# Turns without convolution matmuls behind the scores, and a merge stage written out with its adds moved forward

## The chip, the cores and the metric

The kernel runs on one core of one Trainium2 chip. The metric is the device time of one launch in microseconds; the median of three runs is quoted. A profiled execution has a span, from its first to its last instruction, and a device time of its own, which is a little longer.

## The reference, cut to what matters

One layer of a diffusion backbone over 512 latent tokens and 256 context tokens, model width 1024, all in float32:

```python
h = modulate(rmsnorm(x, norm1_g), sh1, sc1)          # shifts, scales, gates = silu(c) @ w_ada + b_ada
p = h @ w_in                                         # kv | rope key | q | conv x | conv B | conv C | gates
o = mla_latent(qn, qr, keys, rope_keys, values)      # 8 heads, 768 keys, softmax
y_conv = (b_gate * dwconv(c_gate * x_in, conv_w, conv_b)) @ w_conv_out
y_attn = o @ w_attn_out
x = x + g1 * ((sigmoid(gate_attn) * y_attn + sigmoid(gate_conv) * y_conv) @ w_o)
x = x + g2 * conv_ffn(modulate(rmsnorm(x, norm2_g), sh2, sc2), w_up, ffn_conv_w, ffn_conv_b, w_down)
return rmsnorm(x, final_g)
```

The change touches the stage in which attention and the convolution branch (`y_conv` up to the product with `w_conv_out`) run together, and the stage behind it, the gated merge, in which the later shifts, scales and gates (columns of `w_ada` from 2048 on) are summed as well.

## The kernel before, in words

Every product is made of three matmuls (`mm3`, L365 to L369): each operand is split into a rounded part (`hi`) and a rest (`lo`), and hi*hi, lo*hi and hi*lo are summed. Weights come in units of 128 x 1024: SyncE (SP) loads a unit into one of two `raw` buffers, ScalarE (ACT) makes `whi` (`split_hi`, L297), GpSimd (POOL) makes `wlo` (`split_lo`, L306; the subtraction is L311) in one of four slots, TensorE (PE) uses it and counts `w_used`. ACT may split a unit when the one four before it has been used.

**Attention with the convolution.** The 8 heads have 4 query tiles each: 32 turns g, head h = g // 4, tile t = g % 4. In turn g PE does in this order (L1421 to L1439): in turns 3, 11 and 19 first two products that make the keys of the next pair of heads (`keys`), then the scores of turn g + 2 (`scores`; they need the exponential of two turns earlier, since two pairs of banks take turns), a piece of a convolution projection (`conv_piece`, L1403), a third or so of a head's output (`output`, 6 matmuls), and the transposes of the probabilities of turn g (`transposes`, L1387; they need the normalised probabilities and the `lo` halves of turn g - 1). VectorE (DVE) does the maximum (L1011) and the bias (L1013) of turn g + 2, the normalisation (L1018, L1020) of turn g + 1, and the `lo` halves (`ptlo`, L1057 and L1060) of turn g; ACT the `hi` halves (`pthi`, L750 and L753) of turn g, then the exponential (L708) of turn g + 2, then, in some turns, output parts (L716, L721) and a weight split.

The convolution runs beside it in four groups of eight turns, one for each 128 channels. A group has three projections of 24 matmuls, all into PSUM bank 7. Which turn does how many is in `CONV_PIECES` (L84). Between them the bank has to be emptied: `conv_x_copy` on ACT (L726) after the first, `conv_product` on DVE (L1031) after the second, `conv_gate` on DVE (L1045) after the third; `conv_mid` (ACT, L731) and `conv_taps` (DVE, L1035 and L1038) make the depthwise convolution in between. PE waits in `conv_piece`, at the first matmul of each projection, for the copy, the product or the gate before it. `SPLIT_AT` (L85) says behind which turns ACT and POOL split the units of the convolution and the first three of the merge.

**Merge.** For each of 8 blocks d PE does three units of 24 matmuls (L1445 to L1477): the two gates and the two branch outputs. ACT makes the sigmoids (L787), DVE the products (L1096), their sum (L1101), ACT the sum's `hi` copy (L790), DVE its `lo` rest (L1104). ACT has the split of a later unit behind each of the three steps, so also behind its wait for the sum. DVE does four adds of the modulation sum ahead of each block's products (`ada2_add`, L1071; L1080 for the first row block, L1083 after it), each on half a megabyte that SP loads into one of two buffers (`ada2`); SP alternates these loads with those of the next block's units (`load_ada2`, `gate_load`). The loads of `w_o` come behind the last of them. Blocks 0 to 3 are written out, blocks 4 to 7 are a loop with one iteration. Behind the merge PE does the first tile of the product with `w_o`, its last eighth held back until `mlo` of block 7 is there (L1506), and then sums the rows of `adacc` with a matmul by ones (`mod_rows`, L1482).

Of the kernel before, what the change touches and what calls it, by code (L numbers as in the profile page):

```python
# [26 lines left out]
P = 128  # L27
D = 1024
# [55 lines left out]
CONV_PIECES = ((0, 8), (0, 8), (0, 8), (1, 8), (1, 8), (1, 8), (2, 12), (2, 12))  # L84
# [3 lines left out]
def build(nc, x, c, ctx, c_ctx, w_ada, b_ada, norm1_g, w_in, q_norm_g, kv_norm_g, w_uq, w_ukv, conv_w,  # L88
# [3 lines left out]
    with stack:  # L92
# [3 lines left out]
        def sb(name, shape, dt=F32, scope=stack):  # L96
            return scope.enter_context(nc.sbuf_tensor(name, shape, dt))
# [63 lines left out]
        ada2 = sb("ada2", [P, 2, D], scope=mrg)  # L161
        sb("gap2", [P, 1536], scope=mrg)
# [226 lines left out]
        def _(sp):  # L389
# [50 lines left out]
            def load_ada2(n, k, g):  # L440

                wait(sp, s("ada2_used"), n - 1)
                if not isinstance(n, int):
                    sp.sem_inc(s("load_turn"), 1)
                rows = w_ada[k * P:(k + 1) * P, :] if isinstance(k, int) else w_ada[bass.ds(k * P, P), :]
                sp.dma_start(ada2[:, g % 2, :], rows[:, (2 + g) * D:(3 + g) * D]).then_inc(s(f"ada2_loaded{g % 2}"), 16)
# [148 lines left out]
        def _(act):  # L595
# [147 lines left out]
            for g in range(HEADS * TT):  # L743
# [19 lines left out]
                if g % 8 == 2:  # L763
                    conv_x_copy(g // 8)
# [9 lines left out]
            def merge_hi(i, first):  # L774
                for dd in range(4):
                    d = 4 * i + dd
                    b = 4 * (dd % 2)
                    for n in range(3):
                        m = 3 * dd + n
                        if n < 2:  # L780
                            used(act, U_MERGE + 3 * d + n)
                            if first and dd == 0:
                                act.wait_ge(s("z_lo"), CT)
                                act.wait_ge(s("o_lo"), HEADS)
                            if not (first and dd < 2):
                                act.wait_ge(s("m_lo"), d - 1)
                            nc.scalar.activation(work[:, 3 * (dd % 2) + n, :], ps[:, b + n, :], ACT.Sigmoid).then_inc(s("g_sig"), 1)  # L787
                        else:
                            act.wait_ge(s("m_sum"), d + 1)
                            nc.scalar.activation(at1(mhi, d), work[:, 3 * (dd % 2) + 2, :], ACT.Copy).then_inc(s("m_hi"), 1)  # L790
                        split_hi(act, U_MERGE + 12 * i + m + 4, m % SLOTS)

            merge_hi(0, True)
            with act.Fori(1, 2) as i:
                merge_hi(i, False)
# [91 lines left out]
        def _(dve):  # L887
# [183 lines left out]
            def ada2_add(n, k, g):  # L1071

                gg = g * D
                if isinstance(n, int):
                    dve.wait_ge(s(f"ada2_loaded{g % 2}"), 16 * (n // 2 + 1))
                else:
                    dve.wait_ge(s(f"ada2_loaded{g % 2}"), (n - g % 2) * 8 + 16)
                cv = cvec[:, k, 0:1] if isinstance(k, int) else cvec[:, bass.ds(k, 1), 0:1].rearrange("p a b -> p (a b)")
                if isinstance(k, int) and k == 0:
                    nc.vector.tensor_scalar(adacc[:, gg:gg + D], ada2[:, g % 2, :], cv, None, ALU.mult).then_inc(s("ada2_used"), 1)  # L1080
                else:
                    dve.wait_ge(s("ada2_used"), n - 3)
                    nc.vector.scalar_tensor_tensor(out=adacc[:, gg:gg + D], in0=ada2[:, g % 2, :], scalar=cv,  # L1083
                                                   in1=adacc[:, gg:gg + D], op0=ALU.mult, op1=ALU.add).then_inc(s("ada2_used"), 1)


            def merge_lo(i, first):
                for dd in range(4):
                    d = 4 * i + dd
                    b, w = 4 * (dd % 2), 3 * (dd % 2)  # L1090
                    for m in range(4):
                        ada2_add(4 * d + m, d, m)
                    for n in range(2):
                        used(dve, U_MERGE + 3 * d + 2)
                        dve.wait_ge(s("g_sig"), 2 * d + n + 1)
                        nc.vector.tensor_tensor(out=work[:, w + n, :], in0=ps[:, b + 2 + n, :], in1=work[:, w + n, :],  # L1096
                                                op=ALU.mult).then_inc(s("m_prod"), 1)
                    dve.wait_ge(s("m_prod"), 2 * d + 2)
                    if not (first and dd < 2):
                        dve.wait_ge(s("m_lo"), d - 1)  # L1100
                    nc.vector.tensor_tensor(out=work[:, w + 2, :], in0=work[:, w, :], in1=work[:, w + 1, :],  # L1101
                                            op=ALU.add).then_inc(s("m_sum"), 1)
                    dve.wait_ge(s("m_hi"), d + 1)
                    nc.vector.tensor_tensor(out=at1(mlo, d), in0=work[:, w + 2, :], in1=at1(mhi, d).bitcast(F32),  # L1104
                                            op=ALU.subtract).then_inc(s("m_lo"), 1)

            merge_lo(0, True)
            with dve.Fori(1, 2) as i:
                merge_lo(i, False)
# [117 lines left out]
        def _(pe):  # L1227
# [195 lines left out]
            for g in range(HEADS * TT):  # L1423
# [6 lines left out]
                conv_piece(g)  # L1430
# [14 lines left out]
            def merge(i, first):  # L1445
                for dd in range(4):
                    d, b = 4 * i + dd, 4 * (dd % 2)
                    if first and dd == 0:

                        pe.wait_ge(s("p_exp"), HEADS * TT)  # L1450
                    if first and dd == 1:
                        pe.wait_ge(s("pt_lo"), HEADS * TT)
                        pe.wait_ge(s("o_val"), HEADS)
                        pe.wait_ge(s("c_z"), CT)
                    if not (first and dd < 2):
                        pe.wait_ge(s("m_prod"), 2 * d - 2)
                    for n in range(2):
                        m = 3 * dd + n
                        pe.wait_ge(w_lo, U_MERGE + 12 * i + m + 1)
                        project(pe, ps[:, b + n, :], m % SLOTS, hhi, hlo).then_inc(w_used, 1)  # L1460
                    m = 3 * dd + 2
                    slot = m % SLOTS
                    pe.wait_ge(w_lo, U_MERGE + 12 * i + m + 1)
                    if first and dd == 0:
                        pe.wait_ge(s("z_lo"), CT)
                        pe.wait_ge(s("o_lo"), HEADS)
                    for k in range(CT):
                        mm3(pe, ps[:, b + 2, :], (tile_of(whi, slot, k), tile_of(wlo, slot, k)),
                            (qhi[:, 2 * k, :], qlo[:, 2 * k, :]), k == 0, k == CT - 1)
                    for k in range(CT):  # L1470
                        last = mm3(pe, ps[:, b + 3, :], (tile_of(whi, slot, CT + k), tile_of(wlo, slot, CT + k)),
                                   (qhi[:, 2 * k + 1, :], qlo[:, 2 * k + 1, :]), k == 0, k == CT - 1)
                    last.then_inc(w_used, 1)

            merge(0, True)
            with pe.Fori(1, 2) as i:
                merge(i, False)  # L1477
# [181 lines left out]
```

## Time and profile before

| | us |
|---|---|
| median of 3 runs | 907.83 (905.94 to 908.05) |
| the profiled execution | 908.06 |
| its span | 906.3 |

| stage, us from the span's start | PE busy | granted clock |
|---|---|---|
| 45 to 137, projections, queries, values | 77.39 of 92 | 0.91 |
| 137 to 329, attention and convolution | 167.23 of 192 | 0.92 |
| 329 to 350, merge | 21.00 of 21 | 1.00 |
| 350 to 395, merge | 45.00 of 45 | 1.00 |
| 395 to 465, merge and the first tile of w_o | 68.88 of 70 | 1.00 |
| 533 to 770, up projection | 236.69 of 237 | 1.00 |

The page gives over the whole span: PE busy 834.3 us (92%), DVE 498.8 (55%), ACT 377.0 (42%), POOL 368.7 (41%). Busy time says little by itself: one looks for the stages in which PE has gaps or a clock under 1, and then for what ended those gaps. In the rows below, "[2.45 <-DVE tab L1045]" behind an instruction says that its engine sat idle for 2.45 us before it and that DVE's instruction of line 1045 ended that wait. The rounded clock of a stretch mixes the two levels, 2.4 GHz (1.00) and 1.2 GHz (0.50).

### The profile page before, as it was taken

The page shows a single profiled execution, that of the slowest core. Times are in us where ns is not written, and L with a number is a line of the kernel's source. Part 1 is how long each engine was busy: PE and PEld are TensorE (multiplying, and loading weights), DVE is VectorE, ACT ScalarE, POOL GpSimd, SP SyncE. Part 2 cuts the span into 40 slices and gives each one's busy share as a digit, 9 for nine tenths or more (in the row PEclk, how much of TensorE's full clock was granted, in tenths as well). Part 3 has the DMA queues.
Part 4 walks back from the last instruction along what each step waited for, and adds up shares of the span by engine and source line. Part 5 has one row for each costly group of instructions (what it writes and reads, how often), then busy time and mean ns, then how long its engine had stood idle before and what let it go on. Part 6 is the DMA issues. An engine that isn't in the chain of part 4 may idle for free.

```text
span 906.3 us, 11419 instructions
## 1 busy us (share of the span) xinstructions
PE 834.3 (92%) x3960; PEld 685.9 (76%) x3960; DVE 498.8 (55%) x604; ACT 377.0 (42%) x577; POOL 368.7 (41%) x187
## 2 busy tenths in 40 slices
PE   6679969888888799999989989999999999999995
PEld 4458757777777688888857888888888888888884
DVE  5862898776767637877631486655555555100014
ACT  7763445445444442322132445444444444221134
POOL 0193455232433255554453314544444444444420
PEclk9989989999999899999999989999999999999998
DMA  8822212010110138877544213333333332332202
GB/s 313 279 64 53 59 36 71 24 47 24 35 37 24 47 117 250 234 230 237 171 135 160 70 48 93 116 93 93 95 106 100 93 93 93 108 102 93 93 24 93
DMA packets 126238, 96.21 MB, mean 106 GB/s; under 512 B 13468, under 2 KB 111033, under 8 KB 126201
## 3 DMA queue, kind: packets, MB, share of 16 engines
q1 hardware_dynamic: 126169, 95.71, 34.9%
q8 instruction: 23, 0.38, 0.2%
q14 instruction: 14, 0.11, 0.0%
q10 hardware_dynamic: 32, 0.01, 0.0%
HBM read 93.60 MB, written 2.10 MB: 106 GB/s over the span
## 4 chain that ended last, share of the span: by engine, by line
PE 63%; issue 12%; DVE 10%; POOL 6%; DMA 3%; ACT 3%; SPq 1%; POOLq 0%; ACTq 0%; DVEq 0%
PE ps L367 17%; PE ps L369 17%; PE ps L368 17%; PE ps L1416 7%; POOL wlo L311 5%; DVE small L1013 2%; PE ps L1398 2%; PE ps L1387 2%; DMA raw<-w_in_dram 2%; DVE work L988 1%; DVE small L1011 1%; PE ps L1482 1%; POOL ht L511 1%; DVE work L992 1%; DMA xt<-x_dram 1%
## 5 line engine op out<-in xcount | busy, mean ns | idle before, releaser
L311 POOL TENSOR_TENSOR wlo<-raw,whi 128x1024 fp32r<-128x1024 f32 (+2 forms) x130 | 299.7, 2311 | 478.5 <-ACT whi L303 478.4
L367 PE MATMUL ps<-hhi,whi 128*128 128x512 f32 (+1 forms) x552 | 213.3, 386 | 9.0 <-DVE hlo L928 5.8
L368 PE MATMUL ps<-hlo,whi 128*128 128x512 f32 (+1 forms) x552 | 211.9, 384 | 0.0
L369 PE MATMUL ps<-hhi,wlo 128*128 128x512 f32 (+1 forms) x552 | 211.6, 383 | 0.0
L303 ACT ACTIVATE whi<-raw 128x1024 fp32r<-128x1024 f32 (+2 forms) x131 | 127.5, 982 | 129.5 <-PE ps L369 86.7
L367 PEld LDWEIGHTS ps<-hhi,whi 128*128 128x128 f32 x552 | 105.6, 191 | 30.2 <-issue 3.7
L369 PEld LDWEIGHTS ps<-hhi,wlo 128*128 128x128 f32 x552 | 105.6, 191 | 20.1
L368 PEld LDWEIGHTS ps<-hlo,whi 128*128 128x128 f32 x552 | 105.7, 191 | 19.9 <-issue 0.2
L1189 DVE SCALAR_TENSOR_TENSOR work<-ps,prm,work 128x511 f32<-128x511 f32 x44 | 33.0, 749 | 73.5 <-ACT work L851 72.6
L1083 DVE SCALAR_TENSOR_TENSOR adacc<-ada,cvec,adacc 128x1024 f32<-128x1024 f32 x28 | 64.9, 2336 | 14.2 <-DMA ada<-w_ada_dram 14.2
L367 PE MATMUL ps<-fhi,whi 128*128 (+1 forms) x176 | 69.2, 393 | 0.1
L369 PE MATMUL ps<-fhi,wlo 128*128 (+1 forms) x176 | 68.6, 390 | 0.0
L368 PE MATMUL ps<-flo,whi 128*128 (+1 forms) x176 | 68.5, 389 | 0.0
L1212 DVE SCALAR_TENSOR_TENSOR x2T<-ps,mod,x2T 128x512 f32<-128x512 f32 x8 | 6.0, 750 | 107.3 <-PE ps L369 107.3
L851 ACT ACTIVATE work<-ps,prm 128x512 f32<-128x512 f32 x44 | 34.2, 778 | 70.8 <-PE ps L369 70.8
L1416 PE MATMUL ps<-hhi,whi 128*128 128x512 f32 x96 | 44.0, 458 | 20.9 <-DVE work L1031 10.4
L750 ACT ACTIVATE pthi<-ps 128x512 fp32r<-128x512 f32 x32 | 19.1, 598 | 85.9 <-PE ps L1387 85.9
L1198 DVE TENSOR_TENSOR work<-work 128x512 f32<-128x512 f32 x22 | 44.3, 2012 | 8.0 <-ACT work L856 4.2
L1057 DVE TENSOR_TENSOR ptlo<-ps,pthi 128x512 fp32r<-128x512 f32 x32 | 22.0, 687 | 46.4 <-ACT pthi L750 46.4
L1416 PEld LDWEIGHTS ps<-hhi,whi 128*128 128x128 f32 x96 | 21.1, 220 | 29.4 <-issue 24.7
L1416 PE MATMUL ps<-hlo,whi 128*128 128x512 f32 x96 | 42.9, 447 | 0.0
L1416 PE MATMUL ps<-hhi,wlo 128*128 128x512 f32 x96 | 42.3, 441 | 0.0
(235 smaller groups left out, 1477.9 us busy)
## 6 DMA issues: line engine op xcount, KB each, us to landing
raw<-w_up_dram SPq DMA_DIRECT2D x88, 256.0 KB, 3.1
raw<-w_in_dram SPq DMA_DIRECT2D x66, 256.0 KB, 3.4
ada<-w_ada_dram SPq DMA_DIRECT2D x32, 512.0 KB, 4.2
raw<-w_down_dram SPq DMA_DIRECT2D x44, 256.0 KB, 2.7
adaraw<-w_ada_dram SPq DMA_DIRECT2D x32, 256.0 KB, 4.9
raw<-w_o_dram SPq DMA_DIRECT2D x16, 256.0 KB, 3.2
xt<-x_dram SPq DMA_DIRECT2D x4, 512.0 KB, 6.4
raw<-w_attn_out_dram SPq DMA_DIRECT2D x8, 256.0 KB, 2.9
```

Source lines behind the costliest of these rows:

```text
L303: ins = nc.scalar.activation(h, r, ACT.Copy)
L311: ins = (engine or nc.gpsimd).tensor_tensor(out=l, in0=r, in1=h.bitcast(F32), op=ALU.subtract)
L367: pe.matmul(o, l[0], r[0], start=start, stop=False)
L368: pe.matmul(o, l[0], r[1], start=False, stop=False)
L369: return pe.matmul(o, l[1], r[0], start=False, stop=stop)
L750: nc.scalar.activation(pthi[:, 0:4, t * P:(t + 1) * P], ps[:, 4, :].rearrange("p (k n) -> p k n", n=P), ACT.Copy).then_inc(s("pt_hi"), 1)
L851: nc.scalar.activation(work[:, 3 * jj + n, :], ps[:, 2 * jj + n, :], ACT.Identity, bias=col(prm, R_FB + n * FT + j), scale=col(prm, R_FW + ...
L1057: nc.vector.tensor_tensor(out=ptlo[:, 0:4, t * P:(t + 1) * P], in0=ps[:, 4, :].rearrange("p (k n) -> p k n", n=P), in1=pthi[:, 0:4, t * P: ...
L1083: nc.vector.scalar_tensor_tensor(out=adacc[:, gg:gg + D], in0=ada2[:, g % 2, :], scalar=cv, in1=adacc[:, gg:gg + D], op0=ALU.mult, op1=ALU ...
L1189: nc.vector.scalar_tensor_tensor(out=u[:, 1:T], in0=p[:, 0:T - 1], scalar=col(prm, R_FW + n * FT + j), in1=u[:, 1:T], op0=ALU.mult, op1=AL ...
L1198: nc.vector.tensor_tensor(out=work[:, 3 * jj + 2, :], in0=work[:, 3 * jj, :], in1=work[:, 3 * jj + 1, :], op=ALU.mult).then_inc(s("f_prod" ...
L1416: last = pe.matmul(ps[:, 7, :], tile_of(wlo if term == 2 else whi, u % SLOTS, k), (hlo if term == 1 else hhi)[:, k, :], start=i == 0, stop ...
```

## The change

`CONV_PIECES` becomes 12, 12, 0, 12, 12, 0, 24, 0 matmuls, and a turn with 0 skips the call. The bank is emptied in other turns: the copy on ACT behind turn 1 (was 2), the product on DVE at the end of turn 4 (was 5), the taps at the end of turn 6 (as before), the gate at the beginning of turn 7, ahead of that turn's maximum (was at its end). In the merge stage PE, ACT and DVE have their blocks written out instead of half of them in a loop; SP was written out already. The adds of the modulation sum are spread 5, 5, 5, 5, 4, 4, 4, 0 over the blocks instead of four for each, in the same order, and `ada2` has three buffers in place of two.

```diff
-CONV_PIECES = ((0, 8), (0, 8), (0, 8), (1, 8), (1, 8), (1, 8), (2, 12), (2, 12))
+CONV_PIECES = ((0, 12), (0, 12), (0, 0), (1, 12), (1, 12), (1, 0), (2, 24), (2, 0))
+ADA_ADDS = (5, 5, 5, 5, 4, 4, 4, 0)
...
-        ada2 = sb("ada2", [P, 2, D], scope=mrg)
-        sb("gap2", [P, 1536], scope=mrg)
+        ada2 = sb("ada2", [P, 3, D], scope=mrg)
+        sb("gap2", [P, 512], scope=mrg)
...
+            def load_ada2(n):
+
+                k, g = n // 4, n % 4
+                wait(sp, s("ada2_used"), n - 2)
+                sp.dma_start(ada2[:, n % 3, :], w_ada[k * P:(k + 1) * P, (2 + g) * D:(3 + g) * D]).then_inc(s(f"ada2_loaded{n % 3}"), 16)
...
             for d in range(DT):
-                for g in range(4):
-                    load_ada2(4 * d + g, d, g)
-                    if g < 3 and d + 1 < DT:
-                        gate_load(d + 1, g)
+                for m in range(max(3, ADA_ADDS[d])):
+                    if m < ADA_ADDS[d]:
+                        load_ada2(sum(ADA_ADDS[:d]) + m)
+                    if m < 3 and d + 1 < DT:
+                        gate_load(d + 1, m)
...
-                if g % 8 == 2:
+                if g % 8 == 1:
                     conv_x_copy(g // 8)
...
+            for d in range(DT):
+                b, w = 4 * (d % 2), 3 * (d % 2)
+                for n in range(3):
+                    m = 3 * d + n
+                    if n < 2:
+                        used(act, U_MERGE + m)
...
+                        nc.scalar.activation(work[:, w + n, :], ps[:, b + n, :], ACT.Sigmoid).then_inc(s("g_sig"), 1)
+                    else:
+                        act.wait_ge(s("m_sum"), d + 1)
+                        nc.scalar.activation(mhi[:, d, :], work[:, w + 2, :], ACT.Copy).then_inc(s("m_hi"), 1)
+                    split_hi(act, U_MERGE + m + 4, m % SLOTS)
...
             for g in range(HEADS * TT):
                 h, t = g // TT, g % TT
+                if g % 8 == 7:
+                    conv_gate(g // 8)
                 if g + 2 < HEADS * TT:
                     maxima(g + 2)
...
-                if g % 8 in (5, 6, 7):
-                    (conv_product, conv_taps, conv_gate)[g % 8 - 5](g // 8)
+                if g % 8 == 4:
+                    conv_product(g // 8)
+                if g % 8 == 6:
+                    conv_taps(g // 8)
...
+            def ada2_add(n):
+
+                k, gg = n // 4, n % 4 * D
+                dve.wait_ge(s(f"ada2_loaded{n % 3}"), 16 * (n // 3 + 1))
...
+            for d in range(DT):
+                b, w = 4 * (d % 2), 3 * (d % 2)
+                for m in range(ADA_ADDS[d]):
+                    ada2_add(sum(ADA_ADDS[:d]) + m)
+                for n in range(2):
+                    used(dve, U_MERGE + 3 * d + 2)
...
-                conv_piece(g)
+                if CONV_PIECES[g % 8][1]:
+                    conv_piece(g)
...
```

## Rows read from the trace of the kernel before

**Rows 1.** Windows by stage: us, busy time of each engine, PEclk, DMA share, GB/s.
```profile
137.00:329.00 192.00, 167.23 (x903) 141.84 (x902) 135.69 (x219) 91.68 (x171) 66.45 (x34) 0.92 0.14 36
...
350.00:395.00 45.00, 45.00 (x200) 37.28 (x199) 37.75 (x23) 13.42 (x17) 26.64 (x9) 1.00 0.80 238
```

**Rows 2.** The same columns for one group of eight turns.
```profile
231.80:279.46 47.66, 42.06 (x228) 35.59 (x229) 34.59 (x56) 23.02 (x43) 17.19 (x10) 0.93 0.13 34
```

**Rows 3.** Waits of PE, 137 to 329: total us, times, longest.
```profile
PE ps L1416 <- DVE work L1031: 10.4, 4, 3.4
PE ps L1416 <- DVE tab L1045: 7.4, 3, 2.5
PE ps L1416 <- ACT work L726: 3.1, 1, 3.1
```

**Rows 4.** Chain that ended last, in attention: start, us, what.
```profile
184.20 3.59 PE ps L1416 x8
187.79 0.72 PE ps L1398 x6
...
195.19 1.83 PE ps L1416 x8
```

**Rows 5.** Timeline of turns 8 and 9: start, us, engine, line, operation.
```profile
188.35 0.82 PE L1387 MATMUL ps<-ident,work 128*128 128x128 f32 x6
...
189.72 0.28 PE L367 MATMUL ps<-khi,qhi 96*128 96x256 f32 x1
...
190.78 0.39 PE L1416 MATMUL ps<-hhi,wlo 128*128 128x512 f32 x1
```

**Rows 6.** Timeline from transposes of turn 9 to the scores behind the keys.
```profile
192.60 0.82 PE L1387 MATMUL ps<-ident,prob 128*128 128x128 f32 x6
...
196.93 2.40 POOL L311 TENSOR_TENSOR wlo<-raw,whi 128x1024 fp32r<-128x1024 f32 x1 [12.18 <-ACT whi L303]
...
197.44 1.90 DVE L1013 TENSOR_TENSOR small<-small 128x1 f32<-128x1 f32 x1
...
200.51 0.39 PE L367 MATMUL ps<-khi,qhi 96*128 96x256 f32 x1 [0.74 <-ACT prob L708]
```

**Rows 7.** Timeline from transposes of turn 14 to the gate.
```profile
222.34 0.82 PE L1387 MATMUL ps<-ident,work 128*128 128x128 f32 x6
...
223.60 0.69 DVE L1057 TENSOR_TENSOR ptlo<-ps,pthi 128x512 fp32r<-128x512 f32 x1 [4.04 <-ACT pthi L750]
...
225.32 0.75 DVE L1038 SCALAR_TENSOR_TENSOR tab<-work,prm,tab 128x511 f32<-128x511 f32 x1
...
230.98 0.67 DVE L1045 TENSOR_TENSOR tab<-ps,tab 128x512 f32<-128x512 f32 x1
231.10 1.26 POOL L544 TENSOR_TENSOR qlo<-work,qhi 64x512 fp32r<-64x512 f32 x1
```

**Rows 8.** Timeline: transposes of turn 25, and the first merge matmul.
```profile
287.93 0.82 PE L1387 MATMUL ps<-ident,prob 128*128 128x128 f32 x6
...
328.20 0.40 PE L367 MATMUL ps<-hhi,whi 128*128 128x512 f32 x1
```

**Rows 9.** The merge's end: a wait of PE, then timeline rows.
```profile
PE ps L367 <- POOL wlo L311: 1.1, 1, 1.1
...
456.50 1.06 ACT L303 ACTIVATE whi<-raw 128x1024 fp32r<-128x1024 f32 x1 [11.16 <-DMA raw<-w_o_dram]
...
467.79 0.80 PE L367 MATMUL ps<-mhi,whi 128*128 128x512 f32 x1 [2.65 <-DVE mlo L1104]
...
473.58 0.50 PE L367 MATMUL ps<-mhi,whi 128*128 128x512 f32 x1
...
479.24 3.59 PE L1482 MATMUL ps<-adacc,ones 128*1 128x512 f32 x8
```

**Rows 10.** The adds (instructions of a tile: ns min/median/max), and a block's products.
```profile
L1083 DVE SCALAR_TENSOR_TENSOR adacc<-ada,cvec,adacc x28: 1276/2712/3432, 350.3 to 453.8; 128x1024 f32<-128x1024 f32 x28
...
362.50 1.28 DVE L1096 TENSOR_TENSOR work<-ps,work 128x512 f32<-128x512 f32 x2
```

More of the change, by code:

```diff
@@ L438, in _ @@
                                   ukv[:, k, :, 0:NOPE]) for k in range(KVT)])
[L440 to L446, printed above, removed]
+            def load_ada2(n):
+                k, g = n // 4, n % 4
+                wait(sp, s("ada2_used"), n - 2)
+                sp.dma_start(ada2[:, n % 3, :], w_ada[k * P:(k + 1) * P, (2 + g) * D:(3 + g) * D]).then_inc(s(f"ada2_loaded{n % 3}"), 16)
             for j in range(CT):
@@ L772, in _ @@
             split_hi(act, U_MERGE + 3, 3)
[L774 to L795, printed above, removed]
+            for d in range(DT):
[4 more added lines that the diff above has]
+                        used(act, U_MERGE + m)
+                        if d == 0:
+                            act.wait_ge(s("z_lo"), CT)
+                            act.wait_ge(s("o_lo"), HEADS)
+                        wait(act, s("m_lo"), d - 1)
+                        nc.scalar.activation(work[:, w + n, :], ps[:, b + n, :], ACT.Sigmoid).then_inc(s("g_sig"), 1)
[3 more added lines that the diff above has]
+                    split_hi(act, U_MERGE + m + 4, m % SLOTS)
             split_hi(act, U_O + 4, 0)
@@ L1066, in _ @@
                     output_value(h - 1)
-                if g % 8 in (5, 6, 7):
-                    (conv_product, conv_taps, conv_gate)[g % 8 - 5](g // 8)
+                if g % 8 == 4:
+                    conv_product(g // 8)
+                if g % 8 == 6:
+                    conv_taps(g // 8)
             output_value(HEADS - 1)
[L1071 to L1080, printed above, removed]
+            def ada2_add(n):
+                k, gg = n // 4, n % 4 * D
+                dve.wait_ge(s(f"ada2_loaded{n % 3}"), 16 * (n // 3 + 1))
+                if k == 0:
+                    nc.vector.tensor_scalar(adacc[:, gg:gg + D], ada2[:, n % 3, :], cvec[:, k, 0:1], None, ALU.mult).then_inc(s("ada2_used"), 1)
@@ L1081, in ada2_add @@
                 else:
                     dve.wait_ge(s("ada2_used"), n - 3)
-                    nc.vector.scalar_tensor_tensor(out=adacc[:, gg:gg + D], in0=ada2[:, g % 2, :], scalar=cv,
+                    nc.vector.scalar_tensor_tensor(out=adacc[:, gg:gg + D], in0=ada2[:, n % 3, :], scalar=cvec[:, k, 0:1],
                                                    in1=adacc[:, gg:gg + D], op0=ALU.mult, op1=ALU.add).then_inc(s("ada2_used"), 1)
[L1087 to L1105, printed above, removed]
@@ L1107, in _ @@
-            merge_lo(0, True)
-            with dve.Fori(1, 2) as i:
-                merge_lo(i, False)
+            for d in range(DT):
[4 more added lines that the diff above has]
+                    used(dve, U_MERGE + 3 * d + 2)
+                    dve.wait_ge(s("g_sig"), 2 * d + n + 1)
+                    nc.vector.tensor_tensor(out=work[:, w + n, :], in0=ps[:, b + 2 + n, :], in1=work[:, w + n, :],
+                                            op=ALU.mult).then_inc(s("m_prod"), 1)
+                dve.wait_ge(s("m_prod"), 2 * d + 2)
+                wait(dve, s("m_lo"), d - 1)
+                nc.vector.tensor_tensor(out=work[:, w + 2, :], in0=work[:, w, :], in1=work[:, w + 1, :],
+                                        op=ALU.add).then_inc(s("m_sum"), 1)
+                dve.wait_ge(s("m_hi"), d + 1)
+                nc.vector.tensor_tensor(out=mlo[:, d, :], in0=work[:, w + 2, :], in1=mhi[:, d, :].bitcast(F32),
+                                        op=ALU.subtract).then_inc(s("m_lo"), 1)
@@ L1442, in _ @@
                 output(HEADS - 1, 1, part)
[L1445 to L1466, printed above, removed]
-                    for k in range(CT):
[L1468 to L1473, printed above, removed]
@@ L1475, in _ @@
-            merge(0, True)
-            with pe.Fori(1, 2) as i:
-                merge(i, False)
+            for d in range(DT):
+                b = 4 * (d % 2)
+                if d == 0:
+                    pe.wait_ge(s("p_exp"), HEADS * TT)
+                elif d == 1:
+                    pe.wait_ge(s("pt_lo"), HEADS * TT)
+                    pe.wait_ge(s("o_val"), HEADS)
+                    pe.wait_ge(s("c_z"), CT)
+                wait(pe, s("m_prod"), 2 * d - 2)
+                for n in range(2):
+                    m = 3 * d + n
+                    unit(U_MERGE + m)
+                    project(pe, ps[:, b + n, :], m % SLOTS, hhi, hlo).then_inc(w_used, 1)
+                m = 3 * d + 2
+                slot = m % SLOTS
+                unit(U_MERGE + m)
+                if d == 0:
+                    pe.wait_ge(s("z_lo"), CT)
+                    pe.wait_ge(s("o_lo"), HEADS)
+                for n in range(2):
+                    for k in range(CT):
+                        last = mm3(pe, ps[:, b + 2 + n, :], (tile_of(whi, slot, n * CT + k), tile_of(wlo, slot, n * CT + k)),
+                                   (qhi[:, 2 * k + n, :], qlo[:, 2 * k + n, :]), k == 0, k == CT - 1)
+                last.then_inc(w_used, 1)
```

## The prediction

> **What bounds the kernel now.** I read the stages first. Between 137 and 329 us (32 turns of attention) PE is busy 167.2 of 192 us and its mean granted clock is 0.92; in the merge stage behind it PE is busy all the time at clock 1.00 [rows 1]. So there is time to win in the first stage and, until its end, almost none in the second. Then one group of eight turns: 47.66 us, with PE at 0.93 of its clock [rows 2]. The waits of PE name the places: 10.4 us in 4 waits for the convolution's product (L1031), 7.4 in 3 for its gate (L1045), 3.1 once for the copy of its first operand (L726) [rows 3]. All three are the same thing: one PSUM bank (7) takes the convolution's three sums in turn, and PE, in order, stands at the next sum until the bank is emptied. The chain shows the second cost: 8 matmuls behind such a wait take 3.59 us, 8 others 1.83 [rows 4]: half clock, some 1.6 to 1.7 us per stop.
>
> **Yardsticks.** At full clock a 512-column matmul takes 1.83/8 = 0.228 us, six 256-column ones (a third of a head's output, O) 0.72 [rows 4]. Scores S take 190.78-189.72 = 1.06; transposes T and an O together take 189.72-188.35 = 1.37, so T about 0.6 [rows 5]. Two key products are 6x0.228 + 6x0.12 = 2.1. A group is 72x0.228 + 8(1.06+0.57+0.74) + 2.1 = 37.5, about 38.0 with small gaps, so 9.6 of 47.66 us are lost: two stops of 2.3 to 2.5, half clock behind each (1.6 to 1.7), and 0.9 plus 0.4 around the scores behind the keys.
>
> **Attention, part by part.** The matmuls are the same, 24 for each of a group's three sums, only placed 12,12,0,12,12,0,24,0 instead of 8 and 12 at a time. Nothing is added there; what moves is which engine has finished what when PE arrives. I lay the turns out from the starts of transposes T(g), the matmuls at full clock, with these delays from the rows: the first half of ptlo(g) starts T+1.26 and takes 0.69 (223.60-222.34), the taps end T+3.7 (225.32+0.75) [rows 7].
> - *Product (turn 4 to 6).* The product now stands in turn 4, directly behind ptlo(4): about T(4)+3.0. PE goes through O 0.72, S 1.06, T 0.57, O 0.72, S 1.06 before it: T(4) end + 4.1. The 2.3 us stop goes, and its half clock; next late is nothing.
> - *Gate (turn 7 to 8).* It moves ahead of turn 7's maximum and normalisation: ptlo(6), taps, gate end T(6)+4.5, before it came at T+9.3 (230.98+0.67 against 222.34) [rows 7]. PE needs it at T(6)+0.57+1.1+0.74+0.57+1.1 = 4.1: a wait of 0.55 stays. Queued behind the gate on DVE are maxima(9) and normalize(8), then ptlo(7): the next transposes wait for this and for the shared stall below, another 0.5. So 1.1 instead of 2.5 + 1.6.
>  The gate isn't held by POOL, although a POOL operation began before it ended. The Trainium skill (GPSIMD Engine Reference, 1. Specifications) says that the SBUF interfaces are shared and that contention comes with VectorE instructions in a two-port mode or with two SBUF inputs. The gate has one input in PSUM; if it stalled all the same, up to 2.4 us more per group would be lost, and the forecast would be some 7 us later.
> - *Copy (turn 1 to 3).* It goes from turn 2 to turn 1, behind a weight split: T(1)+4.8. With keys in turn 3 PE comes later than that; in the last group, without keys, at T+4.1: a wait of 0.9 for 3.1 [rows 3] + 1.6.
> - *The new loser: scores behind the keys.* Scores S(g+2) of turn 3 wait for the exponential two turns back, that for L1013, and L1013 stands 1.90 us behind POOL's weight split: from T(1) at 192.60 the scores start at 200.51, T+7.9 [rows 6]. This chain hangs on T(1), the split and the exponentials, none of which moves. Before, turn 2's 8 matmuls filled it. Now PE has after T(1): T, O, S, T, keys = 5.2 us of work, and waits 2.7. A wait of 2.5 was followed by half clock [rows 3, 4], so I charge 1.7 for this one too; at nothing if the clock holds.
>
>  A full group is then 7.9 + 1.2 + 2.73 + 0.74 to T(3), 15.4 to T(6) (24 matmuls in it), 13.9 to T(1) of the next: 41.9, and 43.6 with the half clock; 4.0 less than 47.66. Twice: **8.0**. The first group has no output part in turn 1, so less in front of the scores (wait 1.6): it reaches T(9) at 189.2 instead of 192.60: **3.4**. From T(25) at 287.93 to the first merge matmul at 328.20 it was 40.3 [rows 8]; now 9.3 to T(27), 5.1 to T(28), 9.25 to T(30), and 7.15 to the end, since ptlo(31) comes behind taps and gate (wait 0.8, then 2.2, where 0.8 was): 30.8. With half clock at the start of merge, 1.6: **7.9**. Attention in all 19.3. Bounds: 24.4 if no new wait lowers the clock; 12 if every group has one half-clock stretch more (4x1.7).
>
> **Merge.** (a) The loops over one iteration are written out: same instructions, same order; zero on PE, which has no gap there [rows 1]. (b) Five adds per block in the first four. An add takes 1.28 to 3.43 us, mostly 2.7 (POOL's splits again) [rows 10]. DVE is busy 37.75 of the 45 us from 350 on [rows 1]; one more add of about 2.4 per block of 72 matmuls (16.4 us) makes some 44.3 of 45. It just fits. Who waits: ACT stands at each block's sum with the split of a later unit behind it: products of block 1 at 362.50 [rows 10] mean sum 364.5, ACT 366.2, POOL about 369; PE wants that unit at 328.20 + 9x5.45 = 377.3. So 8 us of cover. DMA gets 8 instead of 7 half-megabyte loads per 16.4 us, 256 GB/s where 238 was at 0.80 busy [rows 1]; the third buffer lets SP run one load further ahead, and the weight loads behind the adds' loads in its queue with it. Cost taken: 0 (bounds 0 and 10, the rival below). (c) The last block without adds. Today four loads of ada stand before w_o on SP: ACT gets its first tile at 456.50 after 11.2 us, PE waits 1.1 for it; ACT's sum copy stands behind a further w_o split, mlo is late, and PE waits 2.65 and then works at half clock [rows 9]. With the last load done a block earlier, w_o comes some 10 us earlier. DVE's products, sum and mlo take 3.5 us after PE's last merge unit, and PE has 21 matmuls (4.8) before it needs them. PE's last merge unit ends at 328.20 + 576x0.227 = 458.95, so to the next tile's start at 473.58 it was 14.6; now 24x0.228 + 3.6 (the second four row sums, at full clock [rows 9]) = 9.1. Gain **5.5** (bounds 3 and 6).
>
> **Sum.** 19.3 + 5.5 = 24.8 off the profiled execution's 908.06 (span 906.3): 883.3; its time is 0.2 over the median of 907.83, so **883**.
>
> **The rivals.**
> - *The clock holds* (the waits of 1.6 to 2.7 us don't lower it here): 5 us more, 878. Against it: waits of 2.3 to 2.5 did [rows 3, 4].
> - *DVE can't carry five adds.* At the dearest, 5x3.43 + 3.4 = 20.6 per 16.4 us block; after four blocks 16.8 behind, less 8 of cover, 9 us on PE: 893. For it: 0.98 busy; against: the third buffer takes DMA waits away.
> - *The waits only move.* Each removed stop comes back elsewhere at its price, 9.6 per group, and only the tail is won: 902. For it: the key scores show how. Against: DVE is busy 34.6 of 47.7 us per group [rows 2].
> - *Slower: every empty turn drops the clock.* Turns 2, 5 and 7 leave PE only S, T and an O. If each ends in a wait as long as that at the keys (2.7) with 12 matmuls at half clock (2.6), a group loses 15.9 instead of 9.6: 4x6.3 = 25 lost, 5.5 won, 927. It is slower from 3.7 us per empty turn on. For it: three thin places for two stops. Against: in turns 5 and 7 the counts above leave 0 and 0.55 us. The Trainium skill (TensorE: Matmul & The Clock Gate, A second HAM failure mode: psum-queue depth-cycling) speaks for this rival: frequent short idles between groups of matmuls make the clock swing, with re-warming paid between bursts. In this trace swings stand only behind stops of 2.3 us and more, while the 0.74 in [rows 6] has none.
> - *It does nothing*: matmuls and adds only change place, 908.
>
> **How the numbers follow.** Forecast 0.60 (own range 877 to 890), clock holds 0.12, five adds too many 0.10, waits move 0.08, slower 0.05, nothing 0.03, a still larger gain 0.02. The range 873 to 896 takes in the first three and leaves 0.18 out. About 0.3% can be told from no change by measurement. Faster 0.92, within it 0.03, slower 0.05.
>
> **What would show it.** Right: no PE wait for L1031; waits for L1045 near 0.5; three for the scores behind the keys near 2.7 with a low clock after; group period 43.6; merge gapless, and no wait for mlo or w_o. Wrong: a wait over 2 us in turns 5 to 7 (DVE's or POOL's order misjudged), PE waits for wlo in blocks 3 to 5 (adds), or a group period under 42 with clock 1.00 throughout.

## The result, and the profile after

The kernel after takes **881.65 us** (median of 4 runs, 880.14 to 882.25); the kernel before took 907.94 us beside it (4 runs, 905.94 to 908.87). The ratio is 0.9711, with a 95% interval of 0.969 to 0.9731. The forecast was 883 with a range of 873 to 896. The profiled execution of after has a span of 880.5 us at a mean granted clock of 0.976; before it was 906.3 us at 0.963.

Read the stages first, as before. The window view of after: attention, a stretch of the merge, then two groups of eight turns from transposes to transposes.

```profile
core 0: us, PE busy (x) PEld busy (x) DVE busy (x) ACT busy (x) POOL busy (x), PEclk, DMA share, GB/s
137.00:310.00 173.00, 158.82 (x906) 136.62 (x906) 131.81 (x222) 92.40 (x174) 69.42 (x35) 0.97 0.16 41
320.00:365.00 45.00, 45.00 (x200) 37.28 (x199) 35.03 (x26) 12.84 (x17) 21.75 (x8) 1.00 0.85 266
191.90:235.14 43.24, 40.15 (x230) 34.62 (x229) 33.85 (x57) 22.86 (x43) 17.23 (x9) 0.96 0.14 37
235.14:276.82 41.68, 38.63 (x229) 33.52 (x228) 33.23 (x57) 22.86 (x43) 17.30 (x9) 1.00 0.15 39
```

Attention lost 8.4 us of busy PE time and 10.6 us of idle against the window of 192 us in [rows 1]; the merge stays without a gap. A group fell from 47.66 us [rows 2] to 43.24 and 41.68. The matmuls are the same, so what went is waits and half clock. The waits of PE from 137 to 460 us (in total, times, longest) answer to [rows 3]:

```profile
PE ps L368 <- ACT prob L708: 4.7, 3, 2.5
PE ps L368 <- ACT work L708: 2.5, 1, 2.5
PE ps L1372 <- DVE ptlo L1052: 2.1, 6, 0.6
PE ps L1383 <- DVE ptlo L1055: 1.8, 1, 1.8
...
PE ps L1401 <- DVE tab L1038: 0.9, 3, 0.3
PE ps L1401 <- ACT work L726: 0.7, 1, 0.7
```

The product (L1031 before, L1024 now) is gone from the list, the gate (now L1038) fell from 7.4 to 0.9 us, the copy (L726) from 3.1 to 0.7, and the waits for mlo and w_o at the end of the merge are gone. New are two waits of 2.5 us for the exponential (L708), at the scores behind the keys of turns 11 and 19. At those of turn 3 it is 0.7 us, the second of the three waits in the first line; the third, 1.5 us, is that of the scores at 142 us, which before has too. The timeline around the first (start, us, engine, line, operation, idle time before it), to be read against [rows 6]:

```profile
196.22 2.37 POOL L312 TENSOR_TENSOR wlo<-raw,whi 128x1024 fp32r<-128x1024 f32 x1 [8.04 <-ACT whi L304]
196.74 1.87 DVE L1006 TENSOR_TENSOR small<-small 128x1 f32<-128x1 f32 x1
...
198.64 0.99 ACT L708 ACTIVATE prob<-ps,small 128x768 f32<-128x768 f32 x1 [1.17 <-DVE small L1006]
...
199.77 0.39 PE L368 MATMUL ps<-khi,qhi 96*128 96x256 f32 x1 [2.53 <-ACT prob L708]
...
201.66 0.63 PE L1401 MATMUL ps<-hlo,whi 128*128 128x512 f32 x1
202.09 0.63 PE L1401 MATMUL ps<-hhi,wlo 128*128 128x512 f32 x1
```

The wait is made by one tiny VectorE operation, a bias of 128x1, that begins 0.52 us after POOL's weight split and ends when it does (198.61 for 198.59): 1.87 us, where the same operation takes 0.16 us in other turns (191.75, for one). The exponential stands for it, and the scores two turns on stand for the exponential. Behind this stop 512-column matmuls start 0.43 us apart, at 1.2 GHz. Behind the second, of the same length, they start 0.23 us apart, at 2.4 GHz:

```profile
243.01 0.39 PE L368 MATMUL ps<-khi,qhi 96*128 96x256 f32 x1 [2.52 <-ACT work L708]
...
244.17 0.39 PE L1401 MATMUL ps<-hhi,whi 128*128 128x512 f32 x1
244.40 0.40 PE L1401 MATMUL ps<-hlo,whi 128*128 128x512 f32 x1
```

That is nearly the whole difference between the two groups, 1.56 us, of which 1.52 is busy PE time. The gate of turn 15, against [rows 7]: it is on VectorE at 225.19, between taps and maxima, and PE, which comes a moment early, waits 0.32 us. The split begins in the middle of the gate. The maximum (L1004), which reads PSUM, begins inside the split and takes its usual 0.95 us. What the split holds is again the bias behind it.

```profile
225.19 0.69 DVE L1038 TENSOR_TENSOR tab<-ps,tab 128x512 f32<-128x512 f32 x1
225.50 2.38 POOL L312 TENSOR_TENSOR wlo<-raw,whi 128x1024 fp32r<-128x1024 f32 x1 [8.42 <-ACT whi L304]
225.80 0.95 DVE L1004 TENSOR_REDUCE small<-ps 128x1 f32<-128x768 f32 x1
226.03 0.47 PE L1401 MATMUL ps<-hhi,whi 128*128 128x512 f32 x1 [0.32 <-DVE tab L1038]
226.78 1.11 DVE L1006 TENSOR_TENSOR small<-small 128x1 f32<-128x1 f32 x1
```

**Where the 25.8 us of span went.** From the first scores with a wait (140.43 us before, 142.44 after) to the first merge matmul: 187.77 before, 165.94 after, so 21.8 less. From there to the modulation rows: 141.17 before, 136.77 after, so 4.4 less. The part ahead, which the change doesn't touch, took 2.0 us more in this execution. The part behind took 1.6 less, 0.7 of it still the end of the merge (from the first modulation rows to the next w_o tile 4.21 us before, 3.52 after).

### The profile page after: what moved, and what is told of

It is laid out like the page before. It is cut to its first block, busy times and chain, and to the rows that moved or that the text cites. A ratio compares the mean times of both kernels' runs of the same rounds, so it can differ in the third digit from the quotient of the medians.

```text
span 880.5 us, 11410 instructions
## 1 busy us (share of the span) xinstructions
PE 823.7 (94%) x3960; PEld 679.9 (77%) x3960; DVE 488.6 (55%) x604; ACT 376.1 (43%) x577; POOL 366.5 (42%) x187
## 4 chain that ended last, share of the span: by engine, by line
PE 81%; DVE 8%; issue 3%; ACT 3%; DMA 2%; SPq 1%; POOL 1%; ACTq 0%; DVEq 0%
PE ps L368 23%; PE ps L370 23%; PE ps L369 23%; PE ps L1401 6%; PE ps L1372 2%; PE ps L1383 2%; DVE small L1006 1%; DVE work L981 1%; DMA raw<-w_in_dram 1%; PE ps L1459 1%; DVE work L985 1%; DVE small L1004 1%; POOL ht L511 1%; DMA xt<-ctx_dram 1%; DVE wlo L312 1%
## 5 line engine op out<-in xcount | busy, mean ns | idle before, releaser
L368 PEld LDWEIGHTS ps<-hhi,whi 128*128 128x128 f32 x552 | 105.8, 192 | 32.5 <-DVE hlo L921 5.0
L1076 DVE SCALAR_TENSOR_TENSOR adacc<-ada,cvec,adacc 128x1024 f32<-128x1024 f32 x28 | 63.5, 2311 | 14.3 <-DMA ada<-w_ada_dram 14.3
L1401 PE MATMUL ps<-hhi,whi 128*128 128x512 f32 x96 | 38.7, 403 | 1.6 <-DVE tab L1038 0.9
L368 PEld LDWEIGHTS ps<-fhi,whi 128*128 128x128 f32 x176 | 33.1, 188 | 7.1 <-DVE work L1177 0.5
L370 PEld LDWEIGHTS ps<-fhi,wlo 128*128 128x128 f32 x176 | 33.0, 188 | 7.0
L851 ACT ACTIVATE fhi<-work 128x512 f32 (+1 forms) x22 | 13.9, 633 | 57.2 <-DVE work L1183 57.2
L1401 PE MATMUL ps<-hhi,wlo 128*128 128x512 f32 x96 | 38.2, 398 | 0.0
```

Source lines behind the costliest of these rows:

```text
L368: pe.matmul(o, l[0], r[0], start=start, stop=False)
L370: return pe.matmul(o, l[1], r[0], start=False, stop=stop)
L1401: last = pe.matmul(ps[:, 7, :], tile_of(wlo if term == 2 else whi, u % SLOTS, k), (hlo if term == 1 else hhi)[:, k, :], start=i == 0, stop ...
```

## The experiments

All times are medians beside runs of the kernel before on the same chip (908.57, 909.44 and 908.05 us in the three sets); "attention" is the stretch from the scores at about 142 us to the first merge matmul, "merge" from there to the modulation rows.

### One half of the change alone

a1 is the kernel before with the new convolution pieces, copy, product, taps and gate, its merge in loops with four adds per block and two buffers. a2 is the kernel after with the old pieces and order in attention.

```diff
 # a1: before, with
-CONV_PIECES = ((0, 8), (0, 8), (0, 8), (1, 8), (1, 8), (1, 8), (2, 12), (2, 12))
+CONV_PIECES = ((0, 12), (0, 12), (0, 0), (1, 12), (1, 12), (1, 0), (2, 24), (2, 0))
 # and copy, product, taps and gate as after; a2: after, with these undone
```

> The kernel before with the attention part of the change alone (pieces, copy, product and gate in their new turns); merge stage, its loops, two ada2 buffers and four adds per block as before. Theory (the two parts add up): from the first waiting scores to the first merge matmul some 21.8 us fewer, the wait for mlo and for w_o stay, 886 to 888 us. Rival (part of the attention gain is only there because the merge was mended too, or the merge gives it back since its loads start earlier against other traffic): 891 us or more.

> The changed kernel with the attention part put back as it was before (8,8,8,8,8,8,12,12, copy in turn 2, product in 5, gate at the end of 7). Theory: only the end of the merge gains, 1.1 + 2.7 us of waits and the half clock behind them, 5.7 us: 902 us. Rival (five adds per block cost something that the earlier end of attention hid): 905 us or more.

a1: 883.79 us, ratio 0.9752 (0.9694 to 0.981); attention 164.05 us, merge 140.58. a2: 904.65 us, ratio 0.9954 (0.9935 to 0.9973); attention 187.52, merge 136.11. The halves act apart: a2's attention is that of before, and a1 keeps the wait for mlo at the end of the merge (2.60 us; for w_o it waits 0.35). In after, half clock follows the stop at 142.44 us, which lies in turns where nothing differs; in a1 it doesn't, and its attention is 1.9 us shorter than after's (1.7 of it before T(9)). With 3.8 us more in the merge than after, where 5.5 were expected, that puts it under its expectation. Against before (187.77) the attention part is worth 23.7 us by this pair; the merge part is worth 3.9 by a2's time and 5.1 by its merge stretch. The time lies nearer the rival's 905 than the 902 expected, but no cost of the fifth add shows in the trace: PE has no wait in a2's merge.

### Each of the three stops put back

Each is the kernel after, with one sum's pieces and its bank's emptying as before.

```diff
 # a3: gate last in turn 7 again, behind maxima and normalize
-(2, 24), (2, 0))
+(2, 12), (2, 12))
 # a4: product in turn 5 instead of 4
-(1, 12), (1, 12), (1, 0),
+(1, 8), (1, 8), (1, 8),
 # a5: copy in turn 2 instead of 1
-(0, 12), (0, 12), (0, 0),
+(0, 8), (0, 8), (0, 8),
```

> The changed kernel with the third sum in two pieces of 12 and the gate at the end of turn 7 again. Theory (each bank switch is a stop of its own): in three groups the stop of 2.5 us and 1.6 us of half clock come back in place of 0.3 + 0.2, 10.5 us; in the last group the probabilities' rest is no longer behind the gate, 1.4 us less: 890 to 892 us. Rival (the empty turn 7 is worth little, the gain is one of the whole order): under 885 us.

> The changed kernel with the second sum in three pieces of 8 and the product in turn 5 again. Theory: the stop for the product comes back, 2.3 + 1.7 us in three groups and 3.4 + 2.5 in the last: some 17 us more, 896 to 900 us. Rival: under 885 us.

> The changed kernel with the first sum in three pieces of 8 and the copy in turn 2 again. Theory (the empty turn 2 uncovers the wait of the scores behind the keys, which no bank switch made): that wait falls from 2.5 to some 0.7 us twice, the half clock behind one of them goes, 4.5 to 5 us less; the last group's stop for the copy comes back, 3.1 + 1.6 in place of 0.65 + 0.6, 3.4 us more: 879 to 882 us, no gain from this third of the attention change. Rival (each of the three switches earns about the same): 890 us or more.

a3: 891.0 us (0.9831, 0.9782 to 0.988), attention 172.70. a4: 897.73 (0.9864, 0.9807 to 0.9921), attention 180.52. a5: 880.29 (0.9682, 0.9651 to 0.9713), attention 164.54. The waits of PE in attention, a3's gate, a4's product, and a5's copy with the scores behind the keys:

```profile
PE ps L1401 <- DVE tab L1038: 9.6, 3, 3.2
```

```profile
PE ps L1401 <- DVE work L1024: 10.4, 4, 3.4
```

```profile
PE ps L1372 <- DVE ptlo L1052: 4.0, 4, 1.1
PE ps L1401 <- ACT work L726: 3.1, 1, 3.1
PE ps L368 <- ACT prob L708: 2.3, 2, 1.5
...
PE ps L368 <- ACT work L708: 0.7, 1, 0.7
```

The half clock behind the first stop (142 to 144 us) is none of these three edits' doing. It is there in after and in a4, not in a1, a3 and a5, so a4 is read against after's 165.94 and the other two against a1's 164.05. The product is then worth 14.6 us of attention (16.1 by the medians, 897.73 for 881.65), the gate 8.7 (9.4), and the copy 0.5: nothing that can be told. Together that is 23.8, for a1's 23.7. In a5, turn 2 has its 8 matmuls again, PE reaches the scores behind the keys later and waits 0.7 instead of 2.5; in exchange the transposes of turns 8, 16 and 24 wait 1.1 us each, and the copy's stop is back in the last group. The pieces of the first sum moved that wait in, and the copy's stop out, at about the same price.

### The split that stands before the scores

If the new wait is POOL's split holding the bias on VectorE, then moving the three splits by one turn must take it away. a9 does only that; ACT's half of each of the three units moves with POOL's. a12 is the same kernel again, in a later set.

```diff
-SPLIT_AT = {1: 2, 4: 3, 6: 4, 9: 5, 12: 6, 14: 7, 17: 8, 20: 9, 22: 10, 25: 11, 28: 12, 30: 13, 31: 14}
+SPLIT_AT = {1: 2, 4: 3, 6: 4, 10: 5, 12: 6, 14: 7, 18: 8, 20: 9, 22: 10, 26: 11, 28: 12, 30: 13, 31: 14}
```

> The changed kernel with the weight splits of units 5, 8 and 11 behind turns 10, 18 and 26 in place of 9, 17 and 25. Theory (the scores behind the keys wait because L1006, the bias, stands behind POOL's split): L1006 of turn 10 takes 0.2 in place of 1.9 us, the wait falls from 2.5 to about 1.1, no half clock behind it: 3 to 4 us less, 877 to 879 us. Rival (the wait comes from the depth of the pipeline, exponential to scores, and not from POOL): 881 to 882, L1006 short and the wait as long as before.

> The kernel with the splits at turns 10, 18 and 26 once more, beside its variant on the same chip: 872 to 875 us, with 40.0 us from one group of turns to the next. It is there so that the variant's 1 to 2 us are read against a neighbour and not against a run of another job.

a9: **873.33 us** (0.9621, 0.9587 to 0.9656), attention 156.79. a12: 873.43 us (0.9617, 0.9592 to 0.9642), attention 156.75. The timeline of a9 at the same place:

```profile
194.59 0.16 DVE L1006 TENSOR_TENSOR small<-small 128x1 f32<-128x1 f32 x1
...
194.79 0.99 ACT L708 ACTIVATE prob<-ps,small 128x768 f32<-128x768 f32 x1 [0.55 <-DVE small L1006]
...
195.92 0.39 PE L368 MATMUL ps<-khi,qhi 96*128 96x256 f32 x1 [0.83 <-ACT prob L708]
...
197.75 2.38 POOL L312 TENSOR_TENSOR wlo<-raw,whi 128x1024 fp32r<-128x1024 f32 x1 [11.68 <-ACT whi L304]
...
198.26 1.89 DVE L1006 TENSOR_TENSOR small<-small 128x1 f32<-128x1 f32 x1
```

The bias takes 0.16 us and the wait 0.83. The split now holds the next turn's bias (1.89 us), for which nobody stands, since PE has 12 convolution matmuls there. So the cause is shown, with one thing beside it. The exponential starts 5.03 us behind the start of transposes T(9), in after 6.74: 1.71 less. The bias accounts for 1.17 of that, the time for which ACT sat idle in after. The other 0.54 is ACT's own half of the split (1.06 us), which in after stands ahead of that exponential and has moved as well. The move was worth more than expected: the groups take 39.99 and 39.96 us instead of 43.24 and 41.68, and the last stretch 28.99 instead of 31.56, together 7.5 us. The waits for the copy (0.65) and for the transposes of turn 27 (0.63) went as well, and no half clock is left in attention. Another 1.6 us of a9's shorter attention isn't the move's: from the first scores to T(9) no split moved, and that stretch took 47.85 us for after's 49.46, since its stop at 142 us had no half clock in this execution.

### The order at the end of attention

a10 is a9 with the last taps and the last gate behind the copy of the last probabilities (ptlo of turn 31), not ahead of it.

```diff
-                if g % 8 == 7:
+                if g % 8 == 7 and g < HEADS * TT - 1:
                     conv_gate(g // 8)
...
-                if g % 8 == 6:
+                if g % 8 == 6 and g < HEADS * TT - 2:
                     conv_taps(g // 8)
+                if g == HEADS * TT - 1:
+                    conv_taps(CT - 1)
+                    conv_gate(CT - 1)
```

> The kernel after with POOL's splits moved from turns 9, 17 and 25 to 10, 18 and 26 (as in the run of the split alone, 873.3 us), and in the last group alone the last taps and the gate product issued on VectorE behind the copy of the last probabilities instead of ahead of it. Theory: the wait of the last head's outputs for that copy (1.78 us in the kernel after) is VectorE's order alone, so it falls to 0.1 to 0.9 us and the time to 871 to 873 us. Rival: the last channel tile of the convolution then comes late for the merge, TensorE stands there instead, and the time stays at 873 to 875 us.

a10: **870.86 us** (5 runs, 870.6 to 873.85; ratio 0.9592, 0.9568 to 0.9616), beside a12's 873.43; the intervals overlap, so the step from one to the other isn't shown by the times. The wait is 0.89 us instead of 1.78, attention 155.81 instead of 156.75, and the merge has no gap: 0.9 us is the order's. The rest can't be read off these two times: of the 3.7 us between the two traced executions (872.1 and 875.8) 0.9 is this wait, 1.5 lies at the start of the merge, and 1.3 lies ahead of and behind both stretches, which no edit touches. The first matmul of the merge in a9, then in a12, the same kernel, both behind a wait of 1.78 us:

```profile
298.70 0.40 PE L368 MATMUL ps<-hhi,whi 128*128 128x512 f32 x1
```

```profile
300.05 0.63 PE L368 MATMUL ps<-hhi,whi 128*128 128x512 f32 x1
```

One execution works on at 2.4 GHz, the other at 1.2 for 7 matmuls, and its merge takes 137.63 us against 136.11. Behind the 0.89 us of a10 it takes 136.12.

### What gave the end of the merge its time

a7 is the kernel after with four adds in each block; a11 is a7 with two buffers instead of three, so that only the write-out is left.

```diff
-ADA_ADDS = (5, 5, 5, 5, 4, 4, 4, 0)
+ADA_ADDS = (4, 4, 4, 4, 4, 4, 4, 4)
 # a11 besides: n % 3 becomes n % 2, n - 2 becomes n - 1, at load and add
```

> The changed kernel with four adds in each block again; written-out blocks and three ada2 buffers stay. Theory (the end of merge is won by getting the ada loads and adds out of the last block): both waits at the end come back, 886.5 to 888 us. Rival (the third buffer, which lets the loads of w_o be issued earlier, or the writing out won it): 883 us or less.

> The kernel after with the merge written out, but four adds in each of its eight units and two buffers for their tiles instead of three. Against the run with four adds each and three buffers (885.1 us, merge to modulation rows 138.7 us): if the third buffer is what let w_o be loaded earlier there, the wait for it (1.1 us before) comes back beside the 1.7 to 2.6 us for mlo, merge to modulation rows takes 140 to 141 us and the kernel 887 to 888 us. Rival: the order written out did it by itself; then 138.7 us again and 885 us.

a7: 885.05 us (0.9727, 0.9692 to 0.9761). a11: 886.74 us (0.9762, 0.9738 to 0.9785). Half clock at the merge's start blurs its total, so read the end alone: from the first matmul on mhi to the modulation rows, 9.30 us before, 8.56 in a1, 8.65 in a11, 7.53 in a7, 5.53 in after. The matmul behind the wait for mlo, in a1, a11 and a7 (in after there is no such wait):

```profile
446.21 0.51 PE L367 MATMUL ps<-mhi,whi 128*128 128x512 f32 x1 [2.60 <-DVE mlo L1108]
```

```profile
445.42 0.50 PE L368 MATMUL ps<-mhi,whi 128*128 128x512 f32 x1 [2.68 <-DVE mlo L1093]
```

```profile
446.08 0.50 PE L368 MATMUL ps<-mhi,whi 128*128 128x512 f32 x1 [1.72 <-DVE mlo L1093]
```

Expected for a7 were both waits back; only the one for mlo is. So writing the loops out gives nothing (8.56 and 8.65, and 140.58 and 140.45 us for the whole merge), the third buffer 1.1 us (w_o's first load leaves SP 120.1 us into the merge instead of 121.6), and the last block without adds 2.0. These are readings of single traces: the intervals of a7 and a11 overlap. In after that load leaves 110.3 us into the merge, and mlo is done before PE asks for it:

```profile
418.64 31.10 SPq L248 DMA_DIRECT2D raw<-w_o_dram  x14
...
442.53 0.69 DVE L1093 TENSOR_TENSOR mlo<-work,mhi 128x512 fp32r<-128x512 f32 x1 [0.70 <-ACT mhi L787]
```

### Too many adds

a8 puts eight adds in each of the first four blocks, to find where the rival "DVE can't carry them" begins.

```diff
-ADA_ADDS = (5, 5, 5, 5, 4, 4, 4, 0)
+ADA_ADDS = (8, 8, 8, 8, 0, 0, 0, 0)
```

> The changed kernel with the adds as 8,8,8,8,0,0,0,0. Theory (a block of merge has room for about five adds: DVE was at 0.98 by my count, and 11 loads of half a megabyte per 16.4 us would be 352 GB/s where 266 is the most seen): DVE falls 5 to 6 us behind per block, 8 us of it are covered, PE waits for weights in blocks 2 to 5, 890 to 898 us. Rival (there is room on both): within 1 us of 881.6.

a8: 903.34 us (0.993, 0.9906 to 0.9954), merge 159.6 us. PE's waits from 300 to 470 us, the timeline that leads to the longest of them, the windows view from 306 to 410 us, and what VectorE waited for ahead of its adds (L1076), in the same 104 us:

```profile
PE ps L368 <- POOL wlo L312: 15.9, 3, 7.2
...
357.64 1.28 DVE L1076 SCALAR_TENSOR_TENSOR adacc<-ada,cvec,adacc 128x1024 f32<-128x1024 f32 x1 [1.26 <-DMA ada<-w_ada_dram]
358.84 1.28 DVE L1086 TENSOR_TENSOR work<-ps,work 128x512 f32<-128x512 f32 x2
360.16 0.69 DVE L1090 TENSOR_TENSOR work<-work 128x512 f32<-128x512 f32 x1
360.88 0.63 ACT L787 ACTIVATE mhi<-work 128x512 fp32r<-128x512 f32 x1 [14.21 <-DVE work L1090]
361.42 1.04 ACT L304 ACTIVATE whi<-raw 128x1024 fp32r<-128x1024 f32 x1
362.54 6.41 POOL L312 TENSOR_TENSOR wlo<-raw,whi 128x1024 fp32r<-128x1024 f32 x2 [13.40 <-ACT whi L304]
365.78 0.76 PE L368 MATMUL ps<-hhi,whi 128*128 128x512 f32 x1 [7.19 <-POOL wlo L312]
...
306.00:410.00 104.00, 89.75 (x372) 73.19 (x372) 69.38 (x51) 23.94 (x31) 40.93 (x18) 0.91 0.74 233
...
  DMA ada<-w_ada_dram: 18.7, 13
```

The rival's chain is there, row by row: the last add waits for its tile, then products and sum, then ACT, idle for 14.2 us, with the next split behind its copy of the sum, then POOL's half, and PE stands 7.19 us (and 3.48 and 5.20 later). These 15.9 us are the most of the 22.8 by which the merge is longer; the other 7 are matmuls at half clock behind these stops. But what is short is not VectorE, which is busy 69.4 of 104 us; it stands 18.7 us for the tiles of the adds. That is why a8 came dearer than a sum of add times says: the limit of this move is when the tiles come. SP loads a tile when an add has freed its buffer, and it landed 3.7 to 7.5 us later; whether more buffers or only more bandwidth would help is not shown. In after VectorE stands 14.3 us for tiles of L1076 too, and nobody behind it is late.

## Why the prediction was right

The total was right (881.65 for 883), and the mechanisms of the sum too, but its terms erred in both directions, and that they cancel so well is in part luck. Attention gained 21.8 us for 19.3. The end of the merge gained the 5.7 for 5.5 that is read below, of which 0.65 was lost again to half clock at its start (136.77 us for the 136.12 of a3, a4 and a5, whose merge is the same). What the sum left out, the parts ahead of attention and behind the w_o tile, lost 2.0 and gained 0.9 in the traced execution.

- *Product*: right. No wait for L1024; put back, it costs 14.6 us, four waits of 10.4 in all plus half clock behind two of them.
- *Gate*: forecast 0.55, measured 0.30 to 0.32. The step that it isn't held by POOL holds, though the gate shown above, like the one in [rows 7], began before POOL's operation and so doesn't test it. The gate of turn 31 does: it begins inside a split (303.62 to 306.47) and takes 0.69 us. The transposes behind it (T(8), T(16), T(24)) wait 0.23 us, where 0.5 was taken; that the held bias makes this wait is argued, no run took it away. This is the place where the Trainium skill (GPSIMD Engine Reference, 1. Specifications) was drawn on, and the trace agrees as far as it goes: the gate and the maximum, with an input in PSUM, kept their 0.69 and 0.95 us inside a split, the 128x1 bias, with both inputs in SBUF, took 1.11.

```profile
303.62 2.85 POOL L312 TENSOR_TENSOR wlo<-raw,whi 128x1024 fp32r<-128x1024 f32 x1 [6.40 <-ACT whi L304]
...
304.29 0.69 DVE L1038 TENSOR_TENSOR tab<-ps,tab 128x512 f32<-128x512 f32 x1
```

- *Copy*: forecast wait 0.9, measured 0.65. But it was counted as a gain without its counterpart: with the wait that its pieces bring in at the keys it is worth 0.5 us (a5).
- *Scores behind the keys*: forecast 2.7, measured 2.53 and 2.52, and the cause is the one named (a9): L1013 of before, the bias, is L1006 now. The forecast read it off the trace of before and took it as given: "none of which moves" is true of the change as made, and it left 7.5 us lying there.
- *Half clock behind such a wait*: the mis-sized term. 1.7 us was charged for each of the two, and the first alone got it. A third was charged to the stop ahead of the merge and came; a fourth, behind the stop at 142.44, came and was not charged. Three charged, three come: that is luck. Groups: forecast 43.6 with and 41.9 without it; measured 43.24 and 41.68. Two groups gave 4.4 + 6.0 = 10.4 for a forecast 8.0. (The 15.4 us to T(6) that the forecast called "24 matmuls" has turn 4's 12 in it as well; the length was right, 15.45.)
- *First group* (T(9)): 2.7 for 3.4, because half clock after the stop at 142.44, which before did not have, is in it; without that (a1) it is 4.4. The 1.0 over the forecast is the wait behind the keys of turn 3: 1.6 was taken, 0.66 is measured, so that two waits near 2.7 came and not three. *Last stretch*: 31.56 for 30.8 + 1.6, gain 8.7 for 7.9.
- *Merge, five adds*: cost 0, as forecast, though by a wrong account. VectorE was to be busy 44.3 of 45 us; it was 35.0. The adds' median was 2.05 us where 2.7 was taken, as fewer of them began inside a split: 7 of 14 in that window, 9 of 12 before. One that is running when a split begins takes its 1.28 us (350.26, with a split from 350.65 on). DMA moved 266 GB/s where 256 was forecast.
- *Merge, end*: from PE's last merge unit to the next w_o tile 14.6 us before and 8.9 after, 5.7 for 5.5. w_o came 10.4 us earlier into the merge, for "some 10".

The rivals. *The clock holds* was half true: at the second stop behind the keys it held, at the first it didn't, in every trace that has both. *Waits only move* describes the copy (a5), not the other two. *Every empty turn drops the clock* is out: turns 5 and 7 leave 0 and 0.3 us, and turn 2's wait had half clock once in two. The rule of the Trainium skill that stood behind it (TensorE: Matmul & The Clock Gate, A second HAM failure mode: psum-queue depth-cycling) is not borne out by this case's short idles: the waits of 0.2 to 1.2 us, two or three per group in after and in a5, are followed by 2.4 GHz every time.

## What to carry to other kernels

When an engine in order stands for a bank to be emptied, don't spread its work evenly: finish the sum early, leave one turn empty for the emptying, and check what that turn was covering before. If something is late there, look on VectorE for a one-column operation that is held by a POOL operation for which nobody waits, and move the POOL operation by one turn. The best version here (a10) takes 870.86 us, 10.8 less than the kernel after; a9, with that one move, has 8.3 of them, and in its trace 7.5 lie where a split moved.

## What the runs showed that was not expected

**Half clock behind a stop is not fixed.** In the kernel before, all eight stops of 2.3 us and more in attention are followed by matmuls 0.43 us apart. In the other kernels it depends on more than the stop's length. a2, whose attention is that of before, has it behind seven of its eight. a3 has three stops of 3.2 us at the gate, and only the first is followed by half clock. The first and the third with the matmul behind each (0.63 us against 0.40):

```profile
183.28 0.76 PE L1401 MATMUL ps<-hhi,whi 128*128 128x512 f32 x1 [3.22 <-DVE tab L1038]
183.84 0.63 PE L1401 MATMUL ps<-hlo,whi 128*128 128x512 f32 x1
...
275.74 0.47 PE L1401 MATMUL ps<-hhi,whi 128*128 128x512 f32 x1 [3.21 <-DVE tab L1038]
276.04 0.40 PE L1401 MATMUL ps<-hlo,whi 128*128 128x512 f32 x1
```

In after, a1, a3, a4, a7, a8 and a11 the first 2.5 us stop at the keys has it and the second doesn't, each time. The stop of 1.8 us ahead of the merge has it in one execution of one kernel (a12) and not in the other (a9), and the stop of 1.5 us at 142 us has it in after and not in a11, whose attention is the same. What decides stays open: no run separates what PE did in the turns ahead of a stop from where the stop falls in time. Such a stop is best priced at its own length, with 0 to 1.7 us more behind one of 2.5 us and up to 3 behind those of 3.1 to 3.4 (before at 314.59: twelve matmuls 0.43 us apart).

**A one-column operation can cost as much as a large one.** 128x1 on VectorE took 1.11, 1.87 and 1.89 us when it met POOL's 2.4 us split, for 0.16 alone; each time it ended within 0.03 us of the split. An add of 128x1024 that begins inside a split took up to 3.43 us for 1.28.
